# Streaming the split products of a float32 layer from the last column to the first

## The reference

```python
def swiglu(h, wi, wo):                      # wi 2048 x 11264, wo 5632 x 2048
    g, u = jnp.split(h @ wi, 2, axis=-1)
    return (jax.nn.silu(g) * u) @ wo

xc = ffn_sublayer(xc, sh1, sc1, g1, norm_ffn1_w[l], ffn1_wi[l], ffn1_wo[l])
mq, mk, mv, mo, mg, aq, ak, av, gm, ga = mixer_inputs(xc, sh2, sc2, norm_mix_w[l], w_in[l])
hm, (C_l, n_l, m_l) = mlstm_branch(...)     # bidirectional, 4 heads
ha = context_attention(q, k, v, attn_sink[l])
xc = xc + g2 * merge_branches(hm, ha, gm, ga, w_proj_m[l], w_proj_a[l], w_out[l])
xc = ffn_sublayer(xc, sh3, sc3, g3, norm_ffn2_w[l], ffn2_wi[l], ffn2_wo[l])
```

## Time and profile before

| | |
|---|---|
| time, median of 2 runs | 2427.47 us (2427.22 to 2427.73) |
| span of the profiled execution, first to last instruction | 2427.3 us |
| TensorE busy | 2315.6 us, 95% of the span |
| TensorE weight loads busy (beside the products) | 1798.5 us, 74% |
| VectorE busy | 1249.6 us, 51% |
| ScalarE busy | 931.9 us, 38% |
| mean granted TensorE clock | 0.974 of full speed |
| read from HBM | 543.73 MB, 225 GB/s over the span |

### The profile page before, as it was taken

The page is one execution under the profiler, slowest core; times in us unless marked ns, Lnnn a source line. Parts: engine busy times, 40 slices in busy tenths (PEclk is TensorE's granted clock), DMA queues, the critical chain, the costliest instruction groups (busy, mean ns, idle before and its releaser), DMA issues.

```text
span 2427.3 us, 29221 instructions
## 1 busy us (share of the span) xinstructions
PE 2315.6 (95%) x11108; PEld 1798.5 (74%) x11108; DVE 1249.6 (51%) x1289; ACT 931.9 (38%) x1083; POOL 59.9 (2%) x57
## 2 busy tenths in 40 slices
PE   5699999999999998999977999998999999999998
PEld 0277777777777776777766888787888888888886
DVE  1154455554555547444457455455455555555557
ACT  0253333333333334433445344345434444444442
POOL 0000000000000000000040000000000000000000
PEclk7699999999999998999989999999999999999999
DMA  9969788787787875789611555655555555555553
GB/s 367 330 215 323 253 285 284 253 310 264 280 289 251 304 272 191 277 297 321 231 50 42 185 193 181 202 196 175 186 196 190 190 194 190 189 190 189 191 190 112
DMA packets 273183, 547.86 MB, mean 226 GB/s; under 512 B 9022, under 2 KB 9190, under 8 KB 272880
## 3 DMA queue, kind: packets, MB, share of 16 engines
q1 hardware_dynamic: 193936, 386.36, 46.8%
q10 hardware_dynamic: 76176, 151.15, 17.2%
q0 software_dynamic: 3024, 9.71, 1.4%
HBM read 543.73 MB, written 3.46 MB: 225 GB/s over the span
## 4 chain that ended last, share of the span: by engine, by line
PE 91%; DMA 4%; DVE 3%; ACT 1%; issue 0%; ACTq 0%; DVEq 0%
PE ps L525 27%; PE ps L527 27%; PE ps L526 27%; PE ps L486 5%; DMA ada_w_sb<-in_ada_w 4%; PE ps L512 1%; PE ps L600 1%; DVE w_lo L1145 0%; PE ps L496 0%; ACTq L896 0%; PE ps L749 0%; DVE x L1276 0%; DVE acc L1274 0%; PE ps L834 0%; PE ps L730 0%
## 5 line engine op out<-in xcount | busy, mean ns | idle before, releaser
L1145 DVE TENSOR_TENSOR w_lo<-raw_w,w_hi 128x1024 fp32r<-128x1024 f32 x728 | 895.6, 1231 | 898.6 <-ACT w_hi L885 898.1
L885 ACT CAST w_hi<-raw_w 128x1024 fp32r<-128x1024 f32 x728 | 765.5, 1053 | 1246.1 <-PE ps L527 1210.5
L525 PE MATMUL ps<-w_hi,xT_hi 128*128 128x512 f32 x2080 | 823.1, 396 | 5.1 <-DVE xT_lo L1201 2.6
L527 PE MATMUL ps<-w_hi,xT_lo 128*128 128x512 f32 x2080 | 811.2, 390 | 0.0
L526 PE MATMUL ps<-w_lo,xT_hi 128*128 128x512 f32 x2080 | 811.0, 390 | 0.0
L525 PEld LDWEIGHTS ps<-w_hi,xT_hi 128*128 128x128 f32 x2080 | 391.3, 188 | 115.7 <-issue 29.3
L527 PEld LDWEIGHTS ps<-w_hi,xT_lo 128*128 128x128 f32 x2080 | 391.1, 188 | 83.0
L526 PEld LDWEIGHTS ps<-w_lo,xT_hi 128*128 128x128 f32 x2080 | 391.6, 188 | 77.5
L525 PE MATMUL ps<-w_hi,hT_hi 128*128 128x512 f32 x704 | 276.4, 393 | 5.6 <-DVE hT_lo L1215 5.6
L527 PE MATMUL ps<-w_hi,hT_lo 128*128 128x512 f32 x704 | 275.4, 391 | 0.0
L526 PE MATMUL ps<-w_lo,hT_hi 128*128 128x512 f32 x704 | 275.1, 391 | 0.0
(11 more groups left out here) (225 smaller groups left out, 867.1 us busy)
## 6 DMA issues: line engine op xcount, KB each, us to landing
raw_w<-in_ffn_wi SPq DMA_DIRECT2D x176, 1024.0 KB, 5.1
ada_w_sb<-in_ada_w ACTq DMA_DIRECT2D x144, 1024.0 KB, 9.5
raw_w<-in_ffn_wo SPq DMA_DIRECT2D x88, 1024.0 KB, 5.0
raw_w<-in_w_in SPq DMA_DIRECT2D x68, 1024.0 KB, 5.3
raw_w<-in_w_out SPq DMA_DIRECT2D x16, 1024.0 KB, 5.1
raw_w<-in_w_proj_m SPq DMA_DIRECT2D x8, 1024.0 KB, 5.0
raw_w<-in_w_proj_a SPq DMA_DIRECT2D x8, 1024.0 KB, 5.1
gate_bc<-gate_dram POOLq DMA_DIRECT2D x6, 1024.0 KB, 9.6
```

Source lines behind the costliest of these rows:

```text
L525: pe.matmul(out, a_hi, w_hi[:, slot, kk, :], start=(first and kk == 0), stop=False)
L527: mm = pe.matmul(out, a_lo, w_hi[:, slot, kk, :], start=False, stop=(last and kk == 1))
L885: act.copy(w_hi[:, us % SPL, :, :], raw_w[:, slot, 2 * half:2 * half + 2, :]).then_inc(hi_ready, 1)
L1145: dve.tensor_tensor(w_lo[:, us % SPL, :, :], raw_w[:, slot, 2 * half:2 * half + 2, :], w_hi[:, us % SPL, :, :].bitcast(F32), ALU.subtract) ...
```

## The change

The output and the moving operand of all three split products are addressed with a step of -1 in their innermost dimension: they begin with column 511 and end with column 0. Since operand and output are both reversed, each sum still lands in the column that it had. The stationary operands, the number and the order of the instructions, the semaphores and all other engines' work are as before: instruction by instruction the two programs list alike on every engine (2906 rows on TensorE, 516 on VectorE, 386 on ScalarE, 47 on GpSimd, 180 on SyncE, loops counted once).

```diff
                     for g in range(GROUPS):
                         a_hi = hi[:, kb + kk, g * P:(g + 1) * P]
                         a_lo = lo[:, kb + kk, g * P:(g + 1) * P]
-                        out = ps[:, banks + g, :]
-                        pe.matmul(out, a_hi, w_hi[:, slot, kk, :], start=(first and kk == 0), stop=False)
-                        pe.matmul(out, a_hi, w_lo[:, slot, kk, :], start=False, stop=False)
-                        mm = pe.matmul(out, a_lo, w_hi[:, slot, kk, :], start=False, stop=(last and kk == 1))
+                        out = ps[:, banks + g, ::-1]
+                        pe.matmul(out, a_hi, w_hi[:, slot, kk, ::-1], start=(first and kk == 0), stop=False)
+                        pe.matmul(out, a_hi, w_lo[:, slot, kk, ::-1], start=False, stop=False)
+                        mm = pe.matmul(out, a_lo, w_hi[:, slot, kk, ::-1], start=False, stop=(last and kk == 1))
                 mm.then_inc(units_done, 1)
```

## The result

The changed kernel takes 2474.86 us (median of 2 runs, 2474.68 to 2475.03) against 2427.47 us: a ratio of 1.0196, 95% interval 1.0166 to 1.0225. It is slower by 47.4 us. The span of the profiled execution is 2473.2 us, 45.9 us more than before. A span is not quite the time: this execution was timed at 2475.03 us, 1.8 us above its span, so spans are compared with spans here.

A forecast was written before the change was run, and what follows sets the result against it. TensorE's stream of 8736 split products, 226.8 ns each and 82% of the span, was taken to bound the kernel. The forecast was 2427.3 us + 8736 x 0 = 2427 us, range 2420 to 2560.

The forecast's parts named there:

- What bounds the kernel: Whole kernel: TensorE busy 95% of the span, producers early, so a change in its pace shows almost one to one.
- part (c): Descending writes of the split products into PSUM: taken as nothing, since neighbouring words are still visited in whole groups.
- part (b): Descending fetch of the split products' moving operand: taken as nothing; bounds from 118 us less to half pace.
- Part (a): Start and order of columns in the split products' sums: no new distance between write and next addition, cost 0.
- Rival 1: Split products fetch or write one column at a time, 427.5 ns each: 1753 us added, 4180 us; 17%.
- Rival 2: Extra access or longer start per descending split product, 13.5 ns each: 118 us more, 2545 us; 9%.
- no change: The likeliest case: the split products keep their pace and the kernel stays at 2427 us; 71%.

The follow-up runs named there:

- e3: Kernel before, all steps 1, with xT_hi and xT_lo 32 bytes further, everything else keeping its address modulo 64: 2464.68 us, ratio 1.0153.
- e14: Kernel before, ascending, with a stationary operand that repeats its first column 128 times (step 0): 2447.79 us, ratio 1.0087.
- e5: Changed kernel, operand and output descending, with w_hi 4 bytes further, w_lo 68 and all tiles behind them 128: 2495.60 us, ratio 1.0284.
- e12: Kernel before, all steps 1, with w_hi and w_lo 256 bytes further, hT 448 and hcT 224: 2425.88 us, ratio 0.9997.

## Why the prediction was wrong, point by point

*What bounds the kernel.* Right. The producers absorbed the change, TensorE's pace went into the time almost one to one (46 of some 52 us), no wait took over, and the clock stayed near 0.98.

*The writes into PSUM, part (c).* Right by itself: nothing, shown by the run with the output alone (0.9991 to 1.0010). The Trainium skill's PSUM rule ("Advanced Engine Details and Errata", Memory Cachelines), in the strict reading that would make a descending pattern non-contiguous, does not hold for this step of -1 over float32 columns: 2426.09 us against 2426.52.

*The fetch, part (b).* This is the step that failed: "I take nothing for both", for which the reason was that every group of two or four words is visited whole. That weighs the operand's stream alone, and puts the term at nothing because of the groups, not because of a row. What the runs showed in its place: the fetch loses 6.2 to 6.5 ns per product (operand alone: ratio 1.0206; output alone: 1.0000). The pace depends on how the addresses of the two operands lie to each other: at the relative place at which xT and hT happened to be, 0 modulo 256 bytes, ascending order is the best of everything tried, 226.7 to 227.2 ns, and every kernel in which all three products descend, or walk their blocks downwards, was at 233.3 to 235.6 ns. By the Trainium skill's line rule for SBUF ("Advanced Engine Details and Errata", Memory Cachelines) the change is free; this agrees with the step at half clock (426.7 ns in both directions), and not with the 6.2 to 6.5 ns at full clock. The Trainium skill ("TensorE: Matmul & The Clock Gate", Part 2: What happens when you issue a matmul) says that the loads use a port of their own and that loading the next weights "doesn't steal SBUF read bandwidth from the running matmul". The measured table of places speaks against taking this to mean that the two reads are independent: with the stationary operand xT alone shifted by 32 bytes against the moving one (e3), the kernel is 1.5% slower.

*Part (a)*, no new distance between a write and the next addition: nothing contradicts it, and the output alone cost nothing.

*Rival 1, half pace.* It did not happen: at full clock the pace is 233.3 and not 427 ns.

*Rival 2, a small fixed cost beyond the weight load.* This is what happened, in kind: a cost per product, hidden at half clock, as written there. Its size was set at 13.5 ns, for 2545 us; measured are 6.2 to 6.5 ns on 8352 of 8736 products, 47.4 us. Its mechanism does not hold either: it is no extra access at the start of a descending run (two runs cost what one does, and the order by blocks costs the same without any descending run inside), and no fixed addition to a product, since it is nothing for hcT at a relative place of 32. It was given 9%, and no change 71%, because no row seemed to bear on it.

*The row that was missed.* It stood in the line view of the trace before: the products with hcT take a median of 396 ns where those with xT and hT take 389, with the same instruction, shape, clock and direction. The earlier trace rows shows L525 alone, whose means (396, 393, 395) hide it, since the means of xT and hT contain the products after waits and at half clock. A search for *why* 384 equal instructions were 6.6 ns slower would have shown that a fetch can lose that much through its addresses, and would have put the likely loss at 8352 x 6.6 = 55 us instead of 118.

*Open.* Shown is that the mean pace of ascending products depends on the relative place of the two operands (the readings fit a period of 256 bytes: modulo 512, those at 0 and 256 agree, and those at 128 and 384), and not on where they lie together (a common shift of 32 bytes, the one tried, changes nothing); that the descending loss is in the fetch; and that its size depends on place and on the neighbours. That the weight loads have a part is shown by e3 and e14, where nothing but their operand was moved or changed against the moving one; what inside the memory or the engine collides, and with which product's load, was only argued. Why no tested place (0, 32 and 128) gives a descending operand less than 233.3 ns stays open, and places off the multiples of 32 bytes were tried in e5 alone, descending, where w_hi and w_lo moved by different amounts.

## What to carry to other kernels

The direction in which these products write their output was free; how the moving operand is walked was not, nor was the SBUF layout of either operand. Before changing one of those, compare the step from start to start before and after, for each operand tile by itself: 32 bytes made it 3% longer here, and the time 2%. In a stream of float32r products of 512 columns like this one, try placing the stationary and the moving operands alike modulo 256 bytes. Here all but hcT lie so. Mending hcT alone was not run; e12 takes its 384 products from 233.3 to 226.7 ns, an estimated 384 x 6.6 ns = 2.5 us of 2427, but its other moves make hT slower (229.0 ns), and its time is that of the kernel before (ratio 0.9997). Where like instructions differ in duration, ask for the median by tile: a mean mixes them with the ones after waits.

## What the runs showed of the hardware that was not expected

- The step between float32r products of 512 columns at full clock (213.3 ns of columns) is 226.7 to 227.2 ns in the mean at a relative place of the operands of 0 modulo 256 bytes, 229.0 at 192, 232.5 at 128 and 233.3 at 32, 64 and 224. A shift of everything together by 32 bytes changes none of it.
- Descending writes into PSUM cost nothing; a descending fetch costs 6.2 to 6.5 ns per product at a relative place of 0, 1.6 to 1.8 at 128 and nothing at 32. The slowest steps were 235.6 ns, in e5, with descending operands 4 and 68 bytes further. Walking blocks of 16 columns from the last to the first, ascending inside, costs the same as a full descent.
- At half clock neither shows: 426.7 ns per product in both directions, and at relative places of 0, 128 and 224.
- The product after one of 256 columns starts 117 to 119 ns after it, although the weight load recorded in between lasts 188 ns.
- A stationary operand that repeats one column loads no faster (188 ns), and gives 229.9 ns per product instead of 226.8 to 227.2 at a relative place of 0, and 231.7 instead of 233.3 at 32.
